# Half-size products in the down half of two feed-forward nets: seven in place of eight, with weight sums and remainders made on VectorE

## The reference

```python
# first block
ff = jnp.einsum('bsf,fd->bsd', jnp.square(jax.nn.relu(jnp.einsum('bsd,df->bsf', h, w_ff_in[l]))), w_ff_out[l])
x = layer_norm(DEEPNORM_ALPHA * x + (1.0 + g2) * ff, ln2_g[l], ln2_b[l])
# second block
f = jnp.square(jax.nn.relu(jnp.einsum('bsd,df->bsf', h2, w_mlp1[l])))
x = x + jnp.einsum('bsf,fd->bsd', f, w_mlp2[l])
```

## Time and profile before

| what | value |
|---|---|
| runs of the kernel | 1406.58, 1406.84, 1408.98 us |
| span of the profiled execution | 1405.4 us |
| median less span, taken for what lies around the span | 1.4 us |
| TensorE busy | 1363.7 us (97%) |
| VectorE, GpSimd, ScalarE busy | 706.2, 701.6, 553.1 us |
| first net, about | 553 to 839 us |
| its end and the second block's start | 840 to 850 us |
| second net | 1053.6 to 1402 us |

### The profile page before, as it was taken

How to read it: one execution, slowest core, us unless ns; L and a number is a source line. 1 busy time by engine, 2 the same in 40 slices (tenths; PEclk the granted TensorE clock), 3 DMA queues, 4 the chain that set the end, 5 groups by cost and what they waited for, 6 DMA issues and landing times.

```text
span 1405.4 us, 17541 instructions
## 1 busy us (share of the span) xinstructions
PE 1363.7 (97%) x6663; PEld 1124.5 (80%) x6663; DVE 706.2 (50%) x1023; ACT 553.1 (39%) x825; POOL 701.6 (50%) x556
## 2 busy tenths in 40 slices
PE   2999999999999999999999999999999999999999
PEld 2888778888878788888888887887788888888887
DVE  6676988789753647140324537558624223132221
ACT  0635444576663262241322316325525223232230
POOL 0453854432346666445445545864644544445442
PEclk9999999999999999999999999999999999999999
DMA  9343435655323332322232323242232222322231
GB/s 335 120 119 110 104 120 180 196 152 168 103 76 122 125 115 90 114 96 90 90 103 86 110 90 120 90 125 71 68 98 90 90 90 91 118 90 90 90 107 73
DMA packets 132254, 158.66 MB, mean 113 GB/s; under 512 B 9468, under 2 KB 93712, under 8 KB 131936
## 3 DMA queue, kind: packets, MB, share of 16 engines
q1 hardware_dynamic: 123760, 146.95, 33.0%
q10 hardware_dynamic: 6240, 5.40, 1.6%
q0 software_dynamic: 2192, 5.49, 1.2%
HBM read 153.47 MB, written 2.26 MB: 111 GB/s over the span
## 4 chain that ended last, share of the span: by engine, by line
PE 85%; DVE 5%; POOL 4%; issue 3%; DMA 2%; ACT 1%; SPq 0%; ACTq 0%; POOLq 0%; DVEq 0%
PE bank L1787 25%; PE bank L1789 25%; PE bank L1788 25%; POOL w_lo L582 3%; DVE tmp L1348 2%; PE bank L1986 2%; PE bank L1996 1%; DMA arena<-in_w_ada_dram 1%; PE bank L2179 1%; PE bank L1971 1%; PE bank L2364 1%; PE bank L1999 1%; PE bank L1961 1%; PE bank L2180 1%; DMA a_lo<-arena 1%
## 5 line engine op out<-in xcount | busy, mean ns | idle before, releaser
L582 POOL TENSOR_TENSOR w_lo<-raw,w_hi 128x512 fp32r<-128x512 f32 x420 | 583.4, 1421 | 576.3 <-ACT w_hi L781 576.2
L1787 PE MATMUL bank<-w_hi,a_hi 128*128 128x512 f32 x928 | 364.2, 392 | 4.4 <-POOL w_lo L582 2.2
L1789 PE MATMUL bank<-w_hi,a_lo 128*128 128x512 f32 x928 | 361.4, 389 | 0.0
L1788 PE MATMUL bank<-w_lo,a_hi 128*128 128x512 f32 x928 | 361.2, 389 | 0.0
L781 ACT ACTIVATE w_hi<-raw 128x2048 fp32r<-128x2048 f32 x105 | 200.7, 1911 | 354.6 <-PE bank L1789 350.4
L1787 PE MATMUL bank<-a_hi,w_hi 128*128 128x512 f32 (+1 forms) x832 | 320.8, 386 | 2.9 <-DVE a_lo L1228 1.7
L1789 PE MATMUL bank<-a_hi,w_lo 128*128 128x512 f32 (+1 forms) x832 | 317.1, 381 | 0.0
L1788 PE MATMUL bank<-a_lo,w_hi 128*128 128x512 f32 (+1 forms) x832 | 317.1, 381 | 0.0
L1787 PEld LDWEIGHTS bank<-w_hi,a_hi 128*128 128x128 f32 x928 | 174.2, 188 | 42.1 <-POOL w_lo L582 3.4
L1789 PEld LDWEIGHTS bank<-w_hi,a_lo 128*128 128x128 f32 x928 | 174.2, 188 | 36.6
L1788 PEld LDWEIGHTS bank<-w_lo,a_hi 128*128 128x128 f32 x928 | 174.3, 188 | 35.4
(11 more groups left out here) (253 smaller groups left out, 1288.9 us busy)
## 6 DMA issues: line engine op xcount, KB each, us to landing
raw<-in_w_mlp_dram SPq DMA_DIRECT2D x32, 1024.0 KB, 5.2
raw<-in_w_in_dram SPq DMA_DIRECT2D x24, 1024.0 KB, 5.2
arena<-in_w_ada_dram SPq DMA_DIRECT2D x18, 1024.0 KB, 6.6
raw<-in_w_ff_in_dram SPq DMA_DIRECT2D x16, 1024.0 KB, 5.3
raw<-in_w_ff_out_dram SPq DMA_DIRECT2D x16, 1024.0 KB, 5.0
raw<-in_w_out_dram SPq DMA_DIRECT2D x12, 1024.0 KB, 5.1
raw<-in_w_in_dram SPq DMA_DIRECT2D x16, 512.0 KB, 5.3
arena<-in_w_ada_dram SPq DMA_DIRECT2D x3, 2048.0 KB, 18.1
```

The costliest lines, as they stand in the source:

```text
L582: last = pool.tensor_tensor(w_lo[:, u0 % 2, cols], raw[:, u0 % 2, cols], w_hi[:, u0 % 2, cols].bitcast(F32), ALU.subtract)
L1787: pe.matmul(out_, hi_a, hi_b, start=start, stop=False)
L1788: pe.matmul(out_, hi_a, lo_b, start=False, stop=False)
L1789: return pe.matmul(out_, lo_a, hi_b, start=False, stop=stop)
```

## The change

The quarter's down product is a 512 x 1024 by 1024 x 1024 product. It is now cut in halves each way and computed as seven products of 256 tokens x 512 x 512 (M1, M2, M6, M5, M7, M3, M4, in the order in which they run), in place of eight, from sums and differences of the halves (Strassen, in Winograd's form). A half-size product is 24 matmuls of the helper, so that a quarter has 192 + 168 = 360.

A quarter has eleven weight operations: `c0` to `c3`, the four units of the up weight, and one operand for each product. VectorE makes four sums of weights (T1 to T4, 2048 wide), the sums of squared hidden values (S1 to S4), the low parts of the hidden operands (`split_low`), and `product_lo`, the remainders of the weight operands of all products but M1, in two halves of 1024. GpSimd keeps the remainders of `c0` to `c3` and M1. ScalarE makes the squares and all high parts. Finished products are read twelve at a time of 128 x 512 in a quarter and added to the sums with either sign. M2 stays in PSUM banks 2 and 3 over the four quarters and is read in the last alone. The left half of the down weight has its own buffers (`b11`, `b21`); its right half is loaded into the two `raw` slots, the second of them (`odd`) after GpSimd has finished with `c3`. T2 adds that second half to the first, and stands on VectorE ahead of M2's remainder. The register loops of the two nets are gone; the code is written out. `relative_tiles` stands behind the first two remainders of the second block, and no longer ahead of the first net.

```diff
--- before.py
+++ after.py
+FF_OPS = 11
...
+OP_M1, OP_M2, OP_M6, OP_M5, OP_M7, OP_M3, OP_M4 = range(4, FF_OPS)
+X_BANK, Y_BANK, W_BANK = 6, 4, 2
+PRODUCTS = ((OP_M1, X_BANK, True, 0), (OP_M2, W_BANK, True, 1), (OP_M6, X_BANK, False, 2), (OP_M5, Y_BANK, True, 3),
+            (OP_M7, X_BANK, False, 0), (OP_M3, Y_BANK, False, 1), (OP_M4, X_BANK, False, 2))
...
+        def op_source(u0, n):
+            even, odd = raw[:, u0 % 2], raw[:, (u0 + 1) % 2]
+            return (even, odd, even, odd, b11, b21, b11, t1_sum, even, odd, b21)[n]
...
+            def feed_forward(u0, g0, w1, w2, b_free):
+                for i in range(QUARTERS):
...
+                    down(b21, 1, 0, b_landed[1])
+                    for n in (2, 3):
+                        sp.wait_ge(w_lo_made, u + n - 1)
+                        up(n)
+                    for half in range(2):
+                        sp.wait_ge(w_lo_made, u + half + 3)
+                        down(raw[:, (u0 + half) % 2], half, 1, landed[(u0 + half) % 2])
...
-            relative_tiles()
-            feed_forward(U_FF1, 6)
...
+            def ff_lo(u0, i, n):
+                u, src = u0 + FF_OPS * i + n, op_source(u0, n)
+                pool.wait_ge(w_hi_made, u + 1)
+                for part in range(4):
+                    cols = slice(512 * part, 512 * part + 512)
+                    if part == 3 and n == 0 and i:
+                        pool.wait_ge(w_lo_made, u)
+                    ins = pool.tensor_tensor(w_lo[:, u % 2, cols], src[:, cols], w_hi[:, u % 2, cols].bitcast(F32), ALU.subtract)
...
+            def feed_forward(u0):
+                for i in range(QUARTERS):
+                    for n in range(2 if i == 0 else 0, OP_M2):
+                        ff_lo(u0, i, n)
...
             both_parts(U_QKV2 + 1)
+            relative_tiles()
+            lo(U_QKV2 + 2)
...
+            def feed_forward(u0, g):
...
+                for j in range(KT):
+                    if j in (2, 4, 6):
+                        ff_hi(u0, g, {2: 2, 4: 3, 6: OP_M1}[j])
+                    act.wait_ge(ticks, 2 * u + j + 1)
...
+                    act.activation(rl[:, j % 2], bank[tile_bank(g, j)][:], ACT.Relu).then_inc(relu_read, 1)
+                    act.wait_ge(relu_read, 8 * g + j + 1)
...
+                    act.activation(sq[:, j], rl[:, j % 2], ACT.Square).then_inc(sq_made, 1)
+                    if j == 3:
+                        act.wait_ge(sq_made, 8 * g + 4)
+                        split_high(sq[:, 0:4, 0:256], 0)
...
+            def act_sums(g, ks, signalled):
...
+                for n, dst, a, b in ((S_S1, s1_sum[:, ks], sq[:, ks, down], sq[:, lower, down]), (S_S3, sq[:, ks, down], sq[:, ks, up], sq[:, ks, down]),
+                                     (S_S2, sq[:, ks, up], s1_sum[:, ks], sq[:, ks, up])):
+                    ins = dve.tensor_tensor(dst, a, b, ALU.subtract)
...
+            def product_lo(u0, g, op):
+                u, src = u0 + FF_OPS * (g % QUARTERS) + op, op_source(u0, op)
+                dve.wait_ge(w_hi_made, u + 1)
+                for half in range(2):
+                    cols = slice(1024 * half, 1024 * half + 1024)
+                    dve.tensor_tensor(w_lo[:, u % 2, cols], src[:, cols], w_hi[:, u % 2, cols].bitcast(F32), ALU.subtract)                        .then_inc(w_lo_made if half else prod_lo, 1)
...
+            def feed_forward(u0, g, add, last=None):
...
+                split_low(g, A11, sq[:, 0:4, 0:256], 0)
...
+                dve.tensor_tensor(t1_sum, b11, even, ALU.add).then_inc(t_made, 1)
+                dve.wait_ge(t_made, 4 * g + T_1)
+                dve.wait_ge(landed[(u0 + 1) % 2], slot_landed(u0, i, 5))
+                dve.tensor_tensor(even, even, odd, ALU.add).then_inc(t_made, 1)
+                dve.wait_ge(sq_made, 8 * g + 7)
+                dve.wait_ge(op_lo, SPLITS_Q * g + A11)
+                act_sums(g, slice(0, 3), False)
+                split_low(g, A12A, sq[:, 4:7, 0:256], 1, slice(0, 3))
+                dve.wait_ge(w_lo_made, u + OP_M1 + 1)
+                dve.wait_ge(t_made, 4 * g + T_3)
+                dve.tensor_tensor(b11, b11, even, ALU.add).then_inc(t_made, 1)
+                dve.wait_ge(sq_made, 8 * g + 8)
+                act_sums(g, slice(3, 4), True)
+                split_low(g, A12B, sq[:, 7:8, 0:256], 1, slice(3, 4))
+                product_lo(u0, g, OP_M2)
+                read_product(u, g, READ_M1, OP_M1, add)
+                split_low(g, A_S2, sq[:, 0:4, 0:256], 2)
+                product_lo(u0, g, OP_M6)
...
+                if i == QUARTERS - 1:
+                    read_product(u, g, READ_M2, OP_M2, add, READ_M1)
+                split_low(g, A_S1, s1_sum, 3)
+                product_lo(u0, g, OP_M5)
...
+                product_lo(u0, g, OP_M4)
+                if last:
+                    last(READ_M2)
+                    last(READ_M7)
+                read_product(u, g, READ_M3, OP_M3, add, READ_M6)
+                if last:
+                    last(READ_M3)
+                read_product(u, g, READ_M4, OP_M4, last or add)
...
+            def gated(t, part, dst):
+                link(dve.tensor_tensor(yacc[:, t, part], yacc[:, t, part], row[:, 3, part], ALU.mult))
+                return dve.scalar_tensor_tensor(dst[:, t, part], x1[:, t, part], ALPHA, yacc[:, t, part], ALU.mult, ALU.add)
+            def finish(n):
...
+                for t in (2 * pair, 2 * pair + 1):
...
+                    gated(t, part, x1).then_inc(sum_made, 1)
+                    dve.wait_ge(sum_made, made + t % 2 + 1)
+                    half_stats(t, half, 1 - pair)
...
+            def last_product(t, part, product, negative):
...
+            def product(u0, g, op, b, start, slot):
...
+                free = {OP_M6: READ_M1, OP_M7: READ_M6, OP_M3: READ_M5, OP_M4: READ_M7}
...
+                elif op in free:
+                    pe.wait_ge(c_read, reads(g, free[op]))
...
+                for k in range(4):
+                    if op != OP_M1 and k == 0:
+                        pe.wait_ge(prod_lo, HALVES_Q * g + op - OP_M1)
+                    elif k in (0, 2):
+                        pe.wait_ge(w_lo_made, u + 1)
...
+                    for t in range(2):
+                        a, w = slice(P * t, P * t + P), slice(512 * k, 512 * k + 512)
+                        last = three(bank[b + t][:], high[:, k, a], low[:, k, a], w_hi[:, u % 2, w], w_lo[:, u % 2, w], start and k == 0, k == 3, not start)
+            def feed_forward(u0, g, first):
+                for n in range(first, KT):
+                    up_tile(u0, g, n)
+                for op, b, start, slot in PRODUCTS:
+                    product(u0, g, op, b, start, slot)
```

More of the change, by code:

```diff
@@ L570, in both_parts, with lo @@
                     ins.then_inc(lo_part if part < 3 else w_lo_made, 1)
-            def lo(u0, i=0, per=0, parts=None, turn=None):
+            def lo(u0, i=0, per=0, parts=None, turn=None, root_at=2):
                 pool.wait_ge(w_hi_made, at(i, per, u0 + 1))
                 for part in range(4):
-                    if part == 2 and turn is not None:
+                    if part == root_at and turn is not None:
                         for t in range(2):
@@ new lines, in read_product @@
+            def read_product(u, g, n, op, add, before=None):
+                pair, half = c_block(n)
+                for t in range(2):
+                    dve.wait_ge(ticks, 2 * (u + op) + 1 + t)
+                    if before is not None:
+                        dve.wait_ge(c_read, reads(g, before, t))
+                    add(2 * pair + t, slice(512 * half, 512 * half + 512), bank[PRODUCTS[op - OP_M1][1] + t], n in (READ_M6, READ_M7))
+            def product_lo(u0, g, op):
[4 more added lines that the diff above has]
+                    dve.tensor_tensor(w_lo[:, u % 2, cols], src[:, cols], w_hi[:, u % 2, cols].bitcast(F32), ALU.subtract)                        .then_inc(w_lo_made if half else prod_lo, 1)
```

367 lines of the change are left out of this document (238 added, 129 removed).

## The result

The changed kernel takes 1411.79 us, the median of eight runs (1410.62 to 1413.14), against 1407.61 for the kernel before in the same comparison: a ratio of 1.0029 with a 95% interval of 1.0019 to 1.0039. It is 0.29% slower. The forecast was 1403.5 and, with a chance of 0.51, a faster kernel; the time lies within the range of 1392 to 1415, on the other side of no change. The profiled span is 1409.4 us, 4.0 longer than before.

The account below looks back on a forecast made before the run. TensorE, busy for 97% of the span, was taken as the bound. Terms −20.7 + 2.4 + 12.9 + 2.0 + 0.1 = −3.3 on a span of 1405.4, with 1.4 around it, gave 1403.5 us; range 1392 to 1415.

Parts of the forecast that it names:

- The wait for M2: In each quarter TensorE waits 2.45 us ahead of M2, for a load and then VectorE's list behind it.
- T0: End of `c3`'s remainder on GpSimd, from which a quarter's times were counted; M2 may start 19.0 us later.
- The hold-ups: Ahead of M2, about 2.5 of GpSimd's M1 pieces delay VectorE's list, taking it from 11.3 to 13.8 us.
- rival C: In the product phase VectorE becomes the bound, as successive instructions don't overlap: 12 us more, 1415; chance 0.17.
- The end of the first net: Behind the first net's last products TensorE idles for VectorE's queued blocks, reads and low parts: +12.9 us (8 to 15).
- The stage: From the first net's last matmul to one same matmul of the second block; forecast 12.9 + 2.0 us longer.
- the slow start: At the first net's end TensorE restarts at the lower clock after idling: +2.0 us (0 to 3.6).
- the clock in the quarters: In each quarter's wait for M2 TensorE's clock was taken to hold, so no cost was added.
- rival D: The clock falls in each quarter's wait for M2, at 2.0 us each: 1419 and slower; chance 0.05.
- A gap in the up tiles: Sign that the forecast is wrong: TensorE waiting in a quarter's up tiles because GpSimd is late.
- The extra reads of M2: In each net's last quarter two reads of 0.75 delay M5's and M7's remainders: 1.2 each, +2.4 us (0 to 3.0).
- The tail: Behind the last matmul the second read of M4's two tiles starts 0.07 later: +0.1 us.

Follow-up runs that it names:

- 8: Changed kernel with VectorE gating and adding 8 columns instead of 512 for the four blocks of M2 and M7 at the first net's end; 1408.16 us.
- 3: Changed kernel with 20 transposes of a constant put on TensorE ahead of each M2 but the first; 1407.81 us.
- 2: Changed kernel with four of the first norm's eight gain instructions moved behind `c2`'s remainder, and the first quarter's T1 held until `c3`'s has ended; 1408.29 us.
- 1: Changed kernel with four of the first norm's eight gain instructions moved behind the first split of the first quarter; 1408.79 us.

## Why the prediction was wrong

**The wait for M2 came out as worked out, size and cause.** In the second net's second quarter GpSimd ends `c3`'s remainder at 1175.38 + 6.52 = 1181.90, VectorE resumes with T2 5.06 later, and the first half of M2's remainder ends 18.9 after T0; forecast were 5.2 and 19.0.

```profile
1175.38 6.52 POOL L818 TENSOR_TENSOR w_lo<-raw,w_hi 128x512 fp32r<-128x512 f32 x4 [6.93 <-ACT w_hi L1010]
...
1186.96 2.90 DVE L1508 TENSOR_TENSOR raw<-raw 128x2048 f32<-128x2048 f32 x1 [9.98 <-DMA raw<-in_w_mlp_dram]
1189.78 2.04 DVE L1471 TENSOR_TENSOR tmp<-arena 128x768 f32<-128x768 f32 x1
1191.86 1.93 DVE L1471 TENSOR_TENSOR arena<-arena 128x768 f32<-128x768 f32 x1
...
1199.61 2.35 DVE L1493 TENSOR_TENSOR w_lo<-arena,w_hi 128x1024 fp32r<-128x1024 f32 x2
```

The hold-ups are 0.61 + 1.08 + 0.97 = 2.7 for the 2.5 taken, and two successive remainders take 2.35, spaced by 1.13, so the overlap that rival C doubted is there. A quarter without a fall of the clock is 84.53, for 84.45.

**The end of the first net came out too.** The stage is 14.9 longer than before (87.98 less 73.12), for 12.9 + 2.0, and 8 shows that it is VectorE's work behind M4's remainder, as the step had it. That the sum fits to 0.1 is partly luck: the gaps are 12.3 for 12.9, and the slow start cost 1.9 in matmuls and some 0.9 in the transposes, for the 2.0 taken. The step also had a slip of its own, as 15.8 less 5.44 and 0.5 is 9.9 and not 9.7; the gap is 9.5.

**The step that failed is the clock in the quarters.** The forecast put it at nothing and gave rival D 0.05, because waits of 2.45 lie between long stretches of matmuls and a gap of 1.70 before showed a full clock. The clock fell in four waits of seven, 1.57 us each and 6.3 in all, and with the wait filled (3) in none. The mechanism was among the rivals, its chance was wrong, and its price was between nothing and the 2.0 per quarter of rival D. The rule of the Trainium skill that was named beside D ("TensorE: Matmul & The Clock Gate", section "HAM oscillation — how this bites in real kernels") says in my words that a kernel which waits again and again for the next slice of an operand pays for the clock again and again; the trace agrees, though with four waits in seven and not with each.

Nor was the gap of 1.70 a safe one. The kernel before has a second one ahead of the first net, which stands in every kernel here. In the kernel before:

```profile
491.10 0.36 PE L1787 MATMUL bank<-a_hi,w_hi 128*128 128x256 f32 x1 [1.70 <-DVE a_lo L1228]
```

In the trace of 3 the clock falls behind it, to 0.50 in the window:

```profile
491.93 0.55 PE L2009 MATMUL bank<-a_hi,w_hi 128*128 128x256 f32 x1 [1.70 <-DVE a_lo L1367]
...
492.00:495.00 3.00, 2.91 (x13) 2.64 (x14) 2.82 (x8) 2.18 (x5) 0.99 (x2) 0.50 0.96 310
```

And in 16 of 65 executions of the kernel before that were taken beside the experiments, the mean clock is 0.997 or 0.998, where the others have 0.999 or 1.000, and the time 1408.5 to 1410.3 us for 1406.4 to 1408.4. No trace of these is on record, so which gap it was is not known; but one trace with a full clock could not show that a gap is harmless.

**A step was missing.** The eight instructions of the gain stood in the order ahead of the net, and the prediction didn't follow them, though the change moved the call. A gap in the up tiles was among its signs of being wrong, and this is one. They cost 5.3 in the first quarter's up tiles (2 shows that all of it is theirs); 1.5 of that was not lost twice, as TensorE then came late to M2 and waited 0.8 for it and not 2.3.

**Small terms.** The extra reads of M2 in the last quarters, +2.4 in the sum, cost nothing visible where TensorE came late to M7 by the clock, and 0.7 and 1.1 where it didn't (the gaps in 3). The tail is no longer than it was: from the start of the last matmul to the end of the span 3.65 us, for 3.70 before. What lies around the span is 1.7 (1411.13, the time of the profiled execution, less 1409.4) and not 1.4.

**The sum by parts**, between the two profiled executions, by the starts of the same matmuls:

| part | forecast | measured |
|---|---|---|
| ahead of the first net | 0 | +0.84 |
| first net, to its last matmul | −9.15 | −4.50 |
| the stage at its end | +14.9 | +14.86 |
| from there to the second net | 0 | −0.29 |
| second net | −9.15 | −6.82 |
| behind the last matmul | +0.1 | −0.05 |
| sum | −3.3 | +4.04 |

The 0.84 is there at 50 us already, ahead of all changed code, and is −0.7 in the trace of 1, so nothing is to be read from it. The first net misses by 4.65: two falls of 1.57 and the 5.25 of the gain, less 1.5 and less 1.2 for the reads of M2, are 5.7; about 0.5 of the rest is a wait at 553 us of the kernel before, which the changed one no longer has. The second net misses by 2.33: two falls, less 1.2, and four quarters of 84.53 for 84.45 are 2.3. With the clock held (3) and with the gain out of the way (2) the kernel is 4.0 and 3.5 faster; both together, which was not run, would make 1404.3 for the 1403.5 forecast. That the time lies within the stated range is no merit: its upper end was put there for rival C, and the overlaps that C takes away are there.

## What to carry to other kernels

When work is taken off the bounding engine, ask of every wait that appears not only how long it is but whether the clock holds through it; price the fall with a chance well above nothing, and don't take a gap for harmless because the clock held behind it in one trace. Follow every call that the diff moves, also one beside the change, through what runs beside it at its new place. Where an engine waits for a landing, look in its own list for work that could stand ahead of the wait: here three sums of 512 in each quarter were worth 16.6 us.
